# A decoder layer with product-key experts: one-hots shared out anew, search split, loads moved

## The chip, the core and the metric

The kernel runs on one core of a Trainium2 chip. The metric is the device time of one launch in microseconds (us); lower is better. Before the change it is 3035.75 us (median of 3 runs, 3030.55 to 3037.25).

## The reference

One decoder layer over 1024 tokens of width 1024. Two head groups (multi-scale retention, sliding-window attention) feed an output projection and a layer norm; that part stays as it is. What matters here is the expert layer behind it:

```python
q = (xt @ w_pq).reshape(T, H, 2, PEER_HALF)               # H = 8 heads, 2 halves
s = jnp.einsum('thpd,hpkd->thpk', q, sub_keys)            # 128 keys a half
s1, i1 = lax.top_k(s[:, :, 0], K); s2, i2 = lax.top_k(s[:, :, 1], K)      # K = 16
cand = (s1[..., :, None] + s2[..., None, :]).reshape(T, H, K * K)
top_s, pos = lax.top_k(cand, K)
idx = jnp.take_along_axis(cand_idx, pos, axis=-1)         # i1 * 128 + i2: one of 16384 experts
g = jax.nn.softmax(top_s, axis=-1)
a = gelu(einsum('cd,ced->ce', x, u_tab[idx])) * g         # 128 experts for each token
y = einsum('ce,ced->cd', a, v_tab[idx])
h = layer_norm(ALPHA * h + y, ln2_w, ln2_b)
```

## The kernel before, in words

Five stages follow each other, each with one instruction stream per engine and a meeting of all engines at its end: `project`, `attend`, `score` (product-key scores), `experts_in` (stage four, L1033) and `experts_out` (stage five, L1414). The order of the work is written out by hand; semaphores join the engines, and every engine and queue runs in order.

Instead of gathering 128 rows of u and v for every token, the kernel computes z = u h for all 16384 experts, densely, for five of the eight token blocks (blocks 3 to 7; `ZT` = 640 columns), and a dense gate matrix for six blocks (`GATE_BLOCKS`). The three other blocks get their z by gathered rows of u: GpSimd issues an indirect DMA for each slot, VectorE forms the dot product of the row with h (`dot`, L1360). Two of these blocks gather rows of v in stage five too.

Stage four has eight turns (`for s in range(TB)`) of 32 slots. A slot is half a u tile of 128 experts: TensorE runs 24 matmuls over 384 columns (first half) or 256 columns (second half) of `z_half` (L1178 to 1180). For each tile ScalarE rounds u (`split_u`, L857), GpSimd subtracts (L861), ScalarE copies both halves of z out of PSUM (L1249) and issues the store (L1252). Over that three jobs are spread:

- turns 0 to 5: the search of one token block a turn on VectorE, in pieces (`top_piece`): `side` twice and `pairs` for each head (top 16 of 128, then of 80 sums), `decode` and `names` for two heads. `names` compares (L818), multiplies by the index tables (L822, two instructions of 512 columns) and reduces (L824). `pairs` begins with four small additions (L788). The last heads of blocks 0 and 1 are searched ahead of turn 0.
- all turns: the dots, `PER_TURN` of them in each turn. `gather` runs four slots ahead of `dot` in a ring of six.
- turns 2 to 7: the gate matrix of one block a turn, 32 steps of four tokens in the slots after the first. In a step VectorE makes two one-hots by comparing an iota in PSUM with the expert's two names (`make_hot`, L1348, 1024 columns), ScalarE scales one of them by the gate (`scale_hot`, L1220, four instructions of 128 columns), TensorE multiplies them (L1188) and ScalarE copies the product out (`take_gates`, L1231), storing it every eight steps (L1236). The names and gates of a block come transposed through PSUM in a turn's slot 0 (L1203) and are copied out by VectorE in slot 1 (L1387).

In slot k ScalarE runs, in this order: the split (even slots), the copy of z, the store (odd slots), `scale_hot` of the slot's step, `take_gates` of the step of slot k - 1. TensorE multiplies a step's one-hots behind the half tile of the next slot.

Stage five has 32 rounds. A round takes four rows of z and of v: ScalarE applies Gelu, rounds a and v (L1598, L1603), VectorE multiplies by the gates and forms the low parts (L1707, L1711, L1733), TensorE adds 144 matmuls into y (L1568 to 1570). GpSimd gathers 320 rows (L1638) for VectorE (`add_row`, `dot_row`) in a ring of four. Its first gather waits for the z and gates of round 1 (`pool.wait_ge(z_here[1], 32)`). SP loads v rows 2 and 3, then z and gates of round 1, then h for the cycled blocks, h for the gathered blocks, and v of round 1.

Of the kernel before, what the change touches and what calls it, by code (L numbers as in the profile page):

```python
# [1 line left out]

# [93 lines left out]

def project(nc, d, room):
# [7 lines left out]
    with ExitStack() as ctx:  # L105
        sb, bank, sem = memory(nc, ctx)
        x_raw = room.x_raw
        x_hi = sb("x_hi", [P, KT, T], F32R)
        x_lo = sb("x_lo", [P, KT, T], F32R)
        w_raw = sb("w_raw", [P, KT, 512])  # L110
        w_hi = sb("w_hi", [P, 2, KT, 512], F32R)
        w_lo = sb("w_lo", [P, 2, KT, 512], F32R)
        rope = sb("rope", [P, TB, 2, RD // 2])
        rope64 = sb("rope64", [P, TB, 2, SD // 2])
        t_cos = sb("t_cos", [P, 512])
        t_sin = sb("t_sin", [P, 512])
        res = sb("res", [P, OUT, 512])
# [164 lines left out]
class Ahead:  # L282
# [3 lines left out]
    def __init__(self, nc, ctx):  # L286
        sb, _, sem = memory(nc, ctx)
        self.room = sb("room", [P, 2 * GROUP * T + 2 * D])
        self.taken = 0
# [25 lines left out]
        self.v_here = [sem(f"v_here{e}") for e in range(2)]  # L315
        self.gelu_in, self.prod_in = sem("gelu_in"), sem("prod_in")

    def carve(self, *shape):

        n = int(np.prod(shape))  # L320
        piece = self.room[:, self.taken:self.taken + n]
        self.taken += n
        names = "abc"[:len(shape)]
        return piece.rearrange(f"p ({' '.join(names)}) -> p {' '.join(names)}", **dict(zip(names, shape)))


def attend(nc, d, hT_hi, hT_lo, room, spent):


    with ExitStack() as ctx:  # L330
# [3 lines left out]
        decayT, xi = sb("decayT", [P, RH, P]), sb("xi", [P, RH, P])  # L334
        zeta = sb("zeta", [P, RH])
        masks = sb("masks", [P, 2, 2 * P])
        gn_w, sinks = sb("gn_w", [P, RW]), sb("sinks", [P, QH])
        ln_w, ln_b = sb("ln_w", [P, D]), sb("ln_b", [P, D])
# [5 lines left out]
        rqT, rqxT, rkT = sb("rqT", [P, RH, P]), sb("rqxT", [P, RH, P]), sb("rkT", [P, RH, P])  # L344
        sqT = sb("sqT", [P, QH // 2, P])
        skT = sb("skT", [P, 2, P])
        v_prev = room.carve(SKV)
        kz = sb("kz", [P, RH, P])
        retT = sb("retT", [P, RH, P])
        state = sb("state", [P, RH, P])  # L350
# [394 lines left out]
class TopK:  # L745
# [67 lines left out]
    def names(self, link, b, two):  # L813
# [3 lines left out]
        hs = slice(2 * two, 2 * two + 2)  # L817
        link(nc.vector.tensor_tensor(self.pick[:], bc(self.ab[:].rearrange("p a h k -> p a (h k)"), 3, TOPK),  # L818
                                     bc(bc(self.places[:], 1, 2 * TOPK), 1, 2), ALU.is_equal))
        for a in range(2):  # L820
            pick = self.pick[:, a].rearrange("p (h k) c -> p h k c", k=TOPK)
            last = nc.vector.tensor_tensor(pick, pick, bc(self.top_i[:, b % 2, a, hs], 2, TOPK), ALU.mult)  # L822
# [1049 lines left out]
```

## Time and profile before

| | us |
|---|---|
| median of 3 runs | 3035.75 |
| profiled execution | 3034.71 |
| its span, first to last instruction | 3032.9 |
| TensorE busy | 2833.3 (93%) |
| VectorE busy | 2353.9 (78%) |
| ScalarE busy | 1172.3 (39%) |
| GpSimd busy | 1160.3 (38%) |
| mean DMA rate | 245 GB/s |

Engines are called PE (TensorE), PEld (its weight loads), DVE (VectorE), ACT (ScalarE), POOL (GpSimd) and SP. A busy share is an average over stages with different limits, and issuing a DMA does not count as busy. Matmuls overlap and their ends are modelled, so a matmul's duration is longer than its distance from the next. The bracket behind a row of a timeline is the idle time before it and what ended it. Stage four runs from about 720 to 1938 us, stage five from about 1941 us to the end; turn boundaries are taken where the store of a turn's sixteenth u tile is issued.

### The profile page before, as it was taken

How to read it: one execution, taken by the hardware profiler on the slowest of the kernel's cores; microseconds unless marked ns; L12 is line 12 of the kernel's file. 1: busy time of each engine (PE TensorE's matmuls, PEld its weight loads, DVE VectorE, ACT ScalarE, POOL GpSimd, SP SyncE). 2: the span in 40 equal slices, each digit the busy share in tenths (PEclk: the TensorE clock that was granted, in tenths of full speed). 3: DMA queues.
4: the chain of work that ended last, by engine and by line, in shares of the span. 5: the costliest groups of instructions: out<-in, count | busy, mean ns of one | idle time of the engine just before them, and what ended most of it. 6: DMA issues, size and time to landing. Idle time of an engine off the chain costs nothing. (4 is left out here: it accounts for less than half of the span.)

```text
span 3032.9 us, 42916 instructions
## 1 busy us (share of the span) xinstructions
PE 2833.3 (93%) x15866; PEld 2540.8 (84%) x15866; DVE 2353.9 (78%) x4726; ACT 1172.3 (39%) x2223; POOL 1160.3 (38%) x878
## 2 busy tenths in 40 slices
PE   8997998999789999899999999879999999999998
PEld 7886886888789988888988999868888888888886
DVE  6125774567999998989898777378888888888887
ACT  3112332222122566656665768333233233333331
POOL 4113220002466544444444665233443444444441
PEclk9998999999899999999999999989999999999999
DMA  5214222223788777676777999789999999999991
GB/s 188 102 65 150 87 85 90 70 85 128 244 286 287 259 248 251 243 266 245 272 258 263 366 370 374 263 307 321 331 325 319 326 332 311 327 335 314 332 321 70
DMA packets 311484, 744.31 MB, mean 245 GB/s; under 512 B 22528, under 2 KB 136448, under 8 KB 308096
## 3 DMA queue, kind: packets, MB, share of 16 engines
q1 hardware_dynamic: 190976, 307.68, 30.8%
q0 software_dynamic: 92160, 335.59, 30.6%
q10 hardware_dynamic: 28160, 98.58, 8.1%
q8 instruction: 113, 1.85, 0.2%
q14 instruction: 75, 0.61, 0.1%
HBM read 623.26 MB, written 118.49 MB: 245 GB/s over the span
## 5 line engine op out<-in xcount | busy, mean ns | idle before, releaser
L1568 PE MATMUL y_ps<-v_hi,a_hi 128*128 128x512 f32 x1536 | 601.5, 392 | 27.5 <-DVE a_lo L1711 20.1
L1569 PE MATMUL y_ps<-v_lo,a_hi 128*128 128x512 f32 x1536 | 600.7, 391 | 0.0
L1570 PE MATMUL y_ps<-v_hi,a_lo 128*128 128x512 f32 x1536 | 600.7, 391 | 0.0
L861 POOL TENSOR_TENSOR u_lo<-u_raw,u_hi 128x1024 fp32r<-128x1024 f32 x128 | 307.8, 2404 | 618.5 <-ACT u_hi L857 618.1
L1178 PE MATMUL z_first<-hT_hi,u_hi 128*128 128x384 f32 x1024 | 360.5, 352 | 42.2 <-POOL u_lo L861 39.1
L1638 POOL DMA_INDIRECT v_rows<-in_v,room x176 | 235.8, 1340 | 343.1 <-DVE y L1694 325.2
L1568 PEld LDWEIGHTS y_ps<-v_hi,a_hi 128*128 128x128 f32 x1536 | 290.2, 189 | 89.0 <-DVE a_lo L1711 20.7
L1179 PE MATMUL z_first<-hT_lo,u_hi 128*128 128x384 f32 x1024 | 350.7, 342 | 0.0
L1180 PE MATMUL z_first<-hT_hi,u_lo 128*128 128x384 f32 x1024 | 350.0, 342 | 0.0
L1569 PEld LDWEIGHTS y_ps<-v_lo,a_hi 128*128 128x128 f32 x1536 | 290.2, 189 | 60.3
L1570 PEld LDWEIGHTS y_ps<-v_hi,a_lo 128*128 128x128 f32 x1536 | 290.0, 189 | 60.4
L1220 ACT ACTIVATE hot_g<-hot,gT 128x128 f32<-128x128 f32 x768 | 244.5, 391 | 213.4 <-DVE hot L1348 207.7
L1178 PE MATMUL z_rest<-hT_hi,u_hi 128*128 128x256 f32 x1024 | 297.1, 290 | 0.0
L1180 PE MATMUL z_rest<-hT_hi,u_lo 128*128 128x256 f32 x1024 | 289.6, 283 | 0.0
L1179 PE MATMUL z_rest<-hT_lo,u_hi 128*128 128x256 f32 x1024 | 289.6, 283 | 0.0
L1694 DVE SCALAR_TENSOR_TENSOR y<-v_rows,a_rows,y 128x1024 f32<-128x1024 f32 x176 | 225.7, 1282 | 63.2 <-DMA v_rows<-in_v,room 59.0
L1188 PE MATMUL g_ps<-hot_g,hot 128*128 128x128 f32 x1536 | 212.6, 284 | 64.2 <-ACT hot_g L1220 59.9
L1603 ACT ACTIVATE v_hi<-room 128x1024 fp32r<-128x1024 f32 x128 | 135.8, 1061 | 324.7 <-DMA room<-in_v 320.9
L1348 DVE TENSOR_TENSOR hot<-near,iT 128x1024 f32<-128x1024 f32 x192 | 233.7, 1221 | 33.9 <-PE g_ps L1188 33.5
L1188 PEld LDWEIGHTS g_ps<-hot_g,hot 128*128 128x128 f32 x1536 | 197.5, 197 | 73.3 <-ACT hot_g L1220 66.0
L1178 PEld LDWEIGHTS z_first<-hT_hi,u_hi 128*128 128x128 f32 x1024 | 200.0, 195 | 44.3 <-POOL u_lo L861 40.9
L1360 DVE CUSTOM_DVE_ANT_0 room<-room,h_ps 128x1024 f32<-128x1024 f32 x161 | 196.4, 1220 | 28.0 <-DMA room<-in_u,room 16.5
(213 smaller groups left out, 6033.0 us busy)
## 6 DMA issues: line engine op xcount, KB each, us to landing
u_raw<-in_uT SPq DMA_DIRECT2D x128, 512.0 KB, 4.5
room<-in_v SPq DMA_DIRECT2D x128, 512.0 KB, 7.1
gates<-g_sb ACTq DMA_DIRECT2D x24, 2048.0 KB, 9.8
z<-z_sb ACTq DMA_DIRECT2D x128, 320.0 KB
g_in<-gates SPq DMA_DIRECT2D x16, 1536.0 KB, 18.6
room<-gates SPq DMA_DIRECT2D x15, 1536.0 KB, 19.1
room<-z SPq DMA_DIRECT2D x16, 1280.0 KB, 7.7
z_in<-z SPq DMA_DIRECT2D x16, 1280.0 KB, 7.9
```

The costliest lines, as they stand in the source:

```text
L861: self.nc.gpsimd.tensor_tensor(self.u_lo[e][:], self.u_raw[e][:], self.u_hi[e][:].bitcast(F32), ALU.subtract).then_inc(self.u_lo_in[e], 1)
L1178: nc.tensor.matmul(o, u_hi[e][:, k], hT_hi[:, k, cols], start=(k == 0), stop=False)
L1179: nc.tensor.matmul(o, u_hi[e][:, k], hT_lo[:, k, cols], start=False, stop=False)
L1180: last = nc.tensor.matmul(o, u_lo[e][:, k], hT_hi[:, k, cols], start=False, stop=(k == KT - 1))
L1188: last = nc.tensor.matmul(g_ps[g][:, t], hot[g][:, 1, t], hot1_g[g][:, t], start=True, stop=True)
L1220: last = nc.scalar.activation(hot1_g[g][:, t], hot[g][:, 0, t], ACT.Copy, scale=gT[:, t0 + t:t0 + t + 1])
L1348: nc.vector.tensor_tensor(hot[g][:], bc(bc(iota_ps, 1, 4), 1, 2), bc(iT[:, :, t0:t0 + 4], 3, NK), ALU.is_equal).then_inc(hot_in[g], 1)
L1568: nc.tensor.matmul(o, ah, v_hi[p][:, i, c], start=(opens(r, s) and i == 0), stop=False)
L1569: nc.tensor.matmul(o, ah, v_lo[p][:, i, c], start=False, stop=False)
L1570: last = nc.tensor.matmul(o, al, v_hi[p][:, i, c], start=False, stop=(closes(r, s) and i == GROUP - 1))
L1638: nc.gpsimd.indirect_dma_start(out=rows_in[i % RING][:], out_offset=None, in_=d["u"] if table == "u" else d["v"].rearrange("a b c -> (a b) ...
L1694: nc.vector.scalar_tensor_tensor(y[:, b], rows_in[i % RING][:], a_rows[:, b, slot:slot + 1], y[:, b], ALU.mult, ALU.add).then_inc(row_used, 1)
```

## The change

- Buffers of all stages are cut out of one new tile `late`. No instruction comes or goes with that.
- One-hots: for the first five gate blocks (turns 2 to 6) VectorE makes only the second one-hot (512 columns). ScalarE makes the first one, scaled, by itself: four Abs of name minus iota, a wait for them, and four Relu of gate minus gate times that distance. VectorE copies the negated gates once a turn. The last block (`SIGNED`, turn 7) keeps the old way.
- Search: `pairs` and `names` (now `match` and `weigh`) copy one operand into PSUM and read it there; `weigh` multiplies in one instruction of 1024 columns. In `score` they stay as they were.
- The last head of block 1 is searched in slots 28 to 31 of turn 0, its gates follow in slot 0 of turn 1.
- Dots by turn, and the first slot for them, change; the first four gathers take one slot each.
- Loads: z and gates of round 1 and v rows 2 and 3 are issued at the end of stage four. Stage five's first gathers wait for none of them; v of round 1 is loaded ahead of the gathered blocks' h.

```diff
-    PER_TURN = [40, 40, 34, 34, 34, 34, 60, 44]
+    PER_TURN = [34, 40, 34, 34, 34, 34, 62, 48]
+    SIGNED = DB - 1
...
-            first, end = 6 if s == 0 else 0, 3 * SLOTS // 4 if s == TB - 1 else SLOTS
+            first, end = 8 if s == 0 else 0, 3 * SLOTS // 4 if s == TB - 1 else SLOTS
...
@@ TopK.pairs, TopK.weigh
+        if near is not None:
+            first_side = near[:, NK:NK + TOPK]
+            link(nc.vector.tensor_copy(first_side, self.top[:, 0]))
...
+            link(nc.vector.tensor_copy(top_i, self.top_i[:, b % 2, :, hs]))
+            pick = self.pick[:].rearrange("p a (h k) c -> p (a h) k c", k=TOPK)
+            link(nc.vector.tensor_tensor(pick, pick, bc(top_i.rearrange("p a h c -> p (a h) c"), 2, TOPK), ALU.mult))
...
@@ experts_in, SP: the end of the last turn
+                        sp.dma_start(ahead.g_in1[:], gates[:, :, GROUP * GT:2 * GROUP * GT]).then_inc(ahead.z1_here, 16)
+                        sp.dma_start(ahead.z_in1[:], d["z"].rearrange("n e t -> e n t")[:, GROUP:2 * GROUP]
+                                     ).then_inc(ahead.z1_here, 16)
+                        for e in range(2):
+                            sp.dma_start(ahead.late_rows[e], d["v"][2 + e]).then_inc(ahead.late_v_here[e], 16)
...
@@ experts_in, PE: gates
+                    pe.wait_ge(hot_in[g], step // 2 + 1)
                     pe.wait_ge(hot_g_in[g], step // 2 + 1)
...
@@ experts_in, ACT: scale_hot
-                    act.wait_ge(hot_in[g], step // 2 + 1)
+                    if step // SLOTS == SIGNED:
...
+                    if step % SLOTS == 0:
+                        act.wait_ge(turned, step // SLOTS + 1)
+                    wait(act, g_done[g], step // 2)
                     for t in range(4):
+                        i = t0 + t
+                        last = nc.scalar.activation(apart[g][:, t], iota[:], ACT.Abs, scale=-1.0, bias=iT[:, 0, i:i + 1])
+                    last.then_inc(own_act, 1)
+                    act.wait_ge(own_act, step + 1)
+                    for t in range(4):
+                        i = t0 + t
+                        last = nc.scalar.activation(hot1_g[g][:, t], apart[g][:, t], ACT.Relu,
+                                                    scale=minus_gT[:, i:i + 1], bias=gT[:, i:i + 1])
                     last.then_inc(hot_g_in[g], 1)
...
@@ experts_in, DVE: make_hot (not SIGNED), and slot 1 of a turn
+                        nc.vector.tensor_tensor(hot[g][:], bc(iota_ps, 1, 4), bc(iT[:, 1, t0:t0 + 4], 2, NK),
+                                                ALU.is_equal).then_inc(hot_in[g], 1)
...
+                            nc.vector.tensor_scalar(minus_gT[:], g_ps[0][:, 2], -1.0, None, ALU.mult)
...
@@ experts_out
-                load_v(0, first=2)
-                load_z(1)
                 load_h(slice(GB + 1, TB - 1), cycled_here)
+                load_v(1)
                 load_h(slice(0, GB), rows_here)
-                load_v(1)
...
-                        pool.wait_ge(z_here[1], 32)
                         for k in range(EARLY):
+                            if k == 2:
+                                pool.wait_ge(v_lo_in[0], 2)
+                                pool.wait_ge(v_lo_in[1], 2)
                             gather(k)
```

## Rows read from the trace of the kernel before

**Rows 1.** Stretches: start:end length, then PE, PEld, DVE, ACT, POOL busy; clock, DMA, GB/s.

```profile
720.50:996.00 275.50, 238.67 (x1536) 236.77 (x1536) 258.00 (x800) 62.78 (x100) 151.56 (x112) 0.93 0.79 263
996.00:1645.70 649.70, 587.57 (x4101) 580.96 (x4102) 602.18 (x1521) 393.87 (x834) 290.02 (x205) 0.96 0.72 254
1645.70:1790.30 144.60, 142.68 (x1028) 141.67 (x1028) 109.34 (x154) 100.43 (x210) 92.62 (x74) 1.00 0.96 359
1790.30:1938.40 148.10, 145.05 (x1036) 143.09 (x1035) 96.47 (x134) 100.82 (x215) 76.22 (x58) 1.00 0.89 338
1938.40:2010.00 71.60, 44.53 (x172) 35.70 (x173) 37.79 (x50) 21.41 (x31) 16.23 (x15) 0.82 0.87 313
```

**Rows 2.** Waits in turns 2 to 5: total us, times, longest.

```profile
ACT hot_g L1220 <- DVE hot L1348: 172.3, 96, 6.5
PE g_ps L1188 <- ACT hot_g L1220: 58.0, 16, 5.6
```

**Rows 3.** Groups by line, VectorE, turn 2: count, busy us, mean ns, idle before.

```profile
L1348 DVE TENSOR_TENSOR hot<-near,iT 128x1024 f32<-128x1024 f32 x32 | 39.0, 1220 | 3.6 <-PE g_ps L1188 3.5
L822 DVE TENSOR_TENSOR room<-room,top_i 128x512 f32<-128x512 f32 x8 | 9.6, 1240 | 0.1
```

**Rows 4.** Groups by line, VectorE, turn 0, the same columns.

```profile
L1360 DVE CUSTOM_DVE_ANT_0 room<-room,h_ps 128x1024 f32<-128x1024 f32 x18 | 22.0, 1221 | 1.7 <-DVE top_i L776 0.6
L788 DVE TENSOR_TENSOR room<-top 128x16 f32<-128x16 f32 (+1 forms) x40 | 9.0, 286 | 0.2
L822 DVE TENSOR_TENSOR room<-room,top_i 128x512 f32<-128x512 f32 x12 | 7.8, 689 | 0.2
```

**Rows 5.** Timeline of ScalarE within turn 2: start, us, line, operation.

```profile
1047.99 0.33 ACTq L1236 DMA_DIRECT2D gates<-g_sb  x1
1048.41 1.06 ACT L857 ACTIVATE u_hi<-u_raw 128x1024 fp32r<-128x1024 f32 x1 [0.51 <-ACT g_sb L1231]
1049.38 0.47 ACT L1249 ACTIVATE z_sb<-z_first 128x384 f32<-128x384 f32 x1
1049.79 1.28 ACT L1220 ACTIVATE hot_g<-hot,gT 128x128 f32<-128x128 f32 x4
1050.98 1.09 ACT L1231 ACTIVATE g_sb<-g_ps 128x512 f32<-128x512 f32 x1
1051.94 0.38 ACT L1249 ACTIVATE z_sb<-z_rest 128x256 f32<-128x256 f32 x1
1052.36 0.33 ACTq L1252 DMA_DIRECT2D z<-z_sb  x1
...
1054.97 1.10 ACT L1231 ACTIVATE g_sb<-g_ps 128x512 f32<-128x512 f32 x1
1055.85 1.07 ACT L857 ACTIVATE u_hi<-u_raw 128x1024 fp32r<-128x1024 f32 x1
```

**Rows 6.** One line's instructions: ns min/median/max. L829 (Exp) and L1614 (Gelu) take no pointer.

```profile
L1220 ACT ACTIVATE hot_g<-hot,gT x768: 384/388/412, 1007.1 to 1903.3; 128x128 f32<-128x128 f32 x192
L829 ACT ACTIVATE gap_e<-gap x8: 310/312/314, 730.3 to 1619.5; 128x128 f32<-128x128 f32 x8
L1614 ACT ACTIVATE a_rows<-room x1: 291/291/291, 1951.5 to 1951.5; 128x128 f32<-128x128 f32 x1
```

**Rows 7.** Timeline of TensorE within turn 6: three successive gate steps.

```profile
1702.21 1.05 PE L1188 MATMUL g_ps<-hot_g,hot 128*128 128x128 f32 x8
...
1705.98 1.05 PE L1188 MATMUL g_ps<-hot_g,hot 128*128 128x128 f32 x8
...
1711.04 1.05 PE L1188 MATMUL g_ps<-hot_g,hot 128*128 128x128 f32 x8
```

**Rows 8.** Timeline of VectorE ahead of turn 0: the four additions of one head.

```profile
724.18 0.45 DVE L788 TENSOR_TENSOR room<-top 128x32 f32<-128x32 f32 x4
```

**Rows 9.** Timelines of GpSimd and TensorE early in stage five.

```profile
1960.21 0.96 POOL L1638 DMA_INDIRECT room<-in_v,room  x1 [19.01 <-DMA g_in<-gates]
...
2008.52 0.79 PE L1568 MATMUL y_ps<-v_hi,a_hi 128*128 128x512 f32 x1 [13.96 <-DVE a_lo L1711]
```

**Rows 10.** Line L1638: time from issue to landing of a gather.

```profile
DMA to landing us min/median/max: 4.1/8.0/11.1
```

More of the change, by code:

```diff
@@ L94, in memory, with carve_late, part @@
     return sb, bank, sem
+def carve_late(room, *shapes):
+    ends = list(itertools.accumulate([int(np.prod(shape)) for shape in shapes], initial=0))
+    return [part(room.late[:, a:b], shape) for a, b, shape in zip(ends, ends[1:], shapes)]
+def part(piece, shape):
+    names = "abc"[:len(shape)]
+    return piece.rearrange(f"p ({' '.join(names)}) -> p {' '.join(names)}", **dict(zip(names, shape)))
 def project(nc, d, room):
@@ L1187, in gates @@
                     for t in range(4):
-                        last = nc.tensor.matmul(g_ps[g][:, t], hot[g][:, 1, t], hot1_g[g][:, t], start=True, stop=True)
+                        last = nc.tensor.matmul(g_ps[g][:, t], hot[g][:, t], hot1_g[g][:, t], start=True, stop=True)
                     last.then_inc(g_done[g], 1)
@@ L1300, in _ @@
                             pool.wait_ge(ahead.s_stored, 16 * PH)
-                            for i in range(EARLY):
-                                gather(i)
+                        if s == 0 and 4 <= k < 4 + EARLY:
+                            gather(k - 4)
                         for i in own_rows(s, k):
@@ L1335, in top_piece @@
                         else:
-                            tk.pairs(link, b, h)
+                            tk.pairs(link, b, h, near)
                             if h == PH - 1:
@@ L1433, in experts_out @@
         y = sb("y", [P, TB, D])
-        rows_in = ahead.rows + [sb(f"v_rows{i}", [P, D]) for i in range(RING - len(ahead.rows))]
+        rows_in = ahead.rows + [sb("v_rows", [P, D])] + ahead.late_rows
         a_rows = sb("a_rows", [P, GB, PH * TOPK])
@@ L1439, in experts_out @@
         y_ps = [bank(f"y_ps{n}") for n in range(8)]
-        z_here = [sem(f"z_here{p}") for p in range(2)]
+        z_here = [sem("z0_here"), ahead.z1_here]
         v_here = ahead.v_here
@@ L1484, in closes, with raw @@
             return r == NG - 1 or (s not in HELD and run(r, s) < LAST * (r + 1))
+        def raw(r, i):
+            return ahead.late_rows[i - 2] if r == 0 and i >= 2 else v_raw[i % 2]
         def made(r):
@@ L1529, in load_z, with load_v @@
                         z_here[p], 16)
-                def load_v(r, first=0):
-                    for i in range(first, GROUP):
-                        wait(sp, v_lo_in[i % 2], 2 * r + i // 2)
+                def load_v(r):
+                    for i in range(GROUP):
+                        wait(sp, v_lo_in[i % 2], 1 if r == 1 and i < 2 else 2 * r + i // 2)
                         sp.dma_start(v_raw[i % 2][:], d["v"][GROUP * r + i]).then_inc(v_here[i % 2], 16)
```

150 lines of the change are left out of this document (90 added, 60 removed).

## The prediction

> **What bounds the kernel now.** I read the busy shares by stretch first, then the waits, the groups by line, and the timelines at the places that these named. The change touches stage four and the opening of stage five; the allocation into one tile issues nothing, so stages one to three cost what they cost. In turns 0 and 1 VectorE is busy 258.0 of 275.5 us, and in turns 2 to 5 602.2 of 649.7 us, 162.4 us a turn; TensorE has idle time beside it [rows 1]. Turn 6 has no search: there VectorE is busy 109.3 of 144.6 us, while TensorE is busy 142.7 us at full clock [rows 1]. So 144.6 us is what a turn with a gate block takes when TensorE sets it, and turns 2 to 5 lose 17.8 us each to VectorE. The waits say how: ScalarE waits 172 us for VectorE's one-hots, and TensorE 58 us for the scaled ones [rows 2]. ScalarE itself has room, 98.5 us busy a turn [rows 1]. The change takes from VectorE and gives to ScalarE, so the question is whether ScalarE still has room when it is done.
>
> **VectorE in turns 2 to 6.** A turn has 32 steps; a one-hot instruction falls from 1024 columns, 1.22 us [rows 3], to 512, for which the uncontended product shows 0.69 us [rows 4]: 32 x 0.53 = 17.0 us less. The four pairs of products, eight at 1.24 us [rows 3] (0.69 in turn 0 [rows 4], so they lose time to something else in these turns), become four of 1024 columns at 1.22 plus a small copy, say 0.2: 3.9 us less. Turns 2 to 5 then hold 150.5 - 20.9 = 129.6 us of work, and with the 11.9 us that VectorE idles in such a turn now, 142 us. That is under TensorE's 144.6 us: VectorE stops being the bound.
>
> **ScalarE in turns 2 to 6.** What a tile (two slots, two steps) takes when ScalarE waits for nobody is read start to start [rows 5]: split 0.97, copy 0.41, one-hots 1.19, gates out 0.96, copy 0.42, store 0.42 (as from the gates store to the next split), and for the second step 1.19 and 0.88, with a quarter of a gates store 0.10. Sum 6.54 us; 16 tiles make 104.6 us, room beside 144.6.
>
> A new step: four Abs with one pointer operand, as the four Copy today, 1.28 us to their end [rows 5]; then a wait for their results, for which the nearest row is the 0.04 us from the end of a copy (1051.94 + 0.38) to the store that waits for it [rows 5]; then four Relu with two pointers, scale and bias. One pointer costs 388 - 312 to 388 - 291 = 76 to 97 ns against the same width without [rows 6], about 87. No row shows two. If the second is paid like the first, Relus follow each other at 0.30 + 0.087 = 0.385 us, four take 1.54; if it is free, 1.19. I take 1.54, the nearest row being the price of the first pointer. A step is then 2.86 us instead of 1.19, 1.67 more, and a turn 104.6 + 32 x 1.67 = 158.0 us.
>
> To this comes a gap at each turn's start, since the names of the next block come only after the last product. From the end of the last scaled one-hot TensorE still has a gate block, a wide half, transposes, and a narrow half. Gate block and narrow half are 3.77 us, gate block and wide half 5.06 [rows 7]; with 0.5 for transposes, and 0.8 for ScalarE's copy and store, less the second gate block's 1.05, 9.1 us, against 5.7 us of work that ScalarE has in the meantime (three gates out, two stores and three copies, one split, from the same rows 5). The gap is 3.4 us. With the Exp of 0.31 [rows 6] a turn takes **161.7 us**. ScalarE becomes the bound.
>
> Turns 2 to 5: 4 x 161.7 = 646.8 against 649.7 [rows 1], **-2.9 us**. The seventeen microseconds that VectorE gives up are spent on ScalarE. Turn 6, which VectorE did not hold, goes from 144.6 to 161.7, **+17.1 us**. The doubled wait on TensorE's gate products costs nothing, since VectorE's half is ready first; behind Abs and Relu on ScalarE stand the gates out and the next split, and GpSimd waits for the split, but ScalarE's own sum already counts that.
>
> The Trainium skill, page "ScalarE: Activation LUTs", section "What ACT_TABLE_LOAD costs", says that each such pointer operand adds about 93 ns and that neighbours overlap by about 93 ns. The traces show that for the first pointer only. By it an estimate for the Relus is 1.55 us and the end 3037 us; the case of a free second pointer (below) would be out.
>
> **Turns 0 and 1.** VectorE sets them and does not wait, so only its work counts, not its place: searching block 1's last head later is worth nothing by itself. Six dots fewer at 1.22 [rows 4]: -7.3. The forty additions of turn 0 take 9.0 us [rows 4]; undisturbed a group of four takes 0.45 [rows 8], ten groups 4.5, plus ten copies of 16 columns at some 0.2 (between 0.11, a quarter of that group, and the 0.29 mean of the additions): -2.5. The products: six of 1.22 and a copy against 7.8 us [rows 4], +0.7, and +0.2 in turn 1. Sum **-8.9 us**, between -4 (the copies twice as dear and more, and the dots' gathers starting later) and -14 (part of the 37 us that TensorE idles there [rows 1] goes too). GpSimd's first gathers, one a slot, no longer hold up its u tiles.
>
> **Turn 7.** It keeps the old one-hots and gets four more dots. VectorE has room (96.5 of 148.1 us), the DMAs less: 0.89 busy at 338 GB/s [rows 1]. Four rows are 2.1 MB, 6.2 us at that rate; hidden, 0. I take **+3 us**. Two more in turn 6 find room in the longer turn. The loads added at its end (1.3 + 1.5 + 1.0 MB, four instructions on SP) stand behind the last gates load, when no gather runs any more; SP has nothing else queued. If that cover is gone, 3.8 MB at 338 GB/s are 11 us.
>
> **The opening of stage five.** Until 2010 us TensorE is busy 44.5 of 71.6 us [rows 1]. The first gather waited 19.0 us for round 1's loads and started at 1960.2; the last long wait of TensorE, for round 1's low parts, ends at 2008.5 [rows 9]. VectorE stands between them: ten gathered rows in round 1, each landing 8.0 us after its issue [rows 10] in a ring of four. With the gathers freed at once and round 1's z and v early, VectorE begins that round sooner, but is stopped by the gathered blocks' h, which SP now loads behind v of round 1, whose last row waits for VectorE. Bounds: 0 (h eats it all) and -19 (the gathers' whole head start); half way, a landing of 8 us, is **-8 us**. Behind it TensorE sets the stage as before.
>
> **Sum.** -8.9 - 2.9 + 17.1 + 3 - 8 = +0.3 us on the profiled execution's 3034.71 (span 3032.9 and 1.8 around it): 3035.0. The median of the runs lies 1.0 above that execution; I say **3035**. A difference of 0.2%, 6 us, is what a measurement of this kernel can tell from none.
>
> **The rivals.**
> - *The second pointer is free.* Step 2.51, +1.32; a turn 104.6 + 42.2 + 3.7 = 150.5, say 151 with VectorE and TensorE close behind: turns 2 to 5 -45.7, turn 6 +6.4, the rest -13.9, together -53: **2982**. For it: only that no row shows two. Chance 0.16.
> - *Slower: the wait between Abs and Relu is dear.* ScalarE must let its last Abs land before the first Relu, 160 times. My 0.04 us is from a store behind a copy, not from an arithmetic instruction behind its own kind. At 0.20 it adds 160 x 0.16 = 26: **3061**. It decides from 0.08 us on. Against it: the four Copy of today follow each other without any such gap [rows 5], but none of them reads the one before. Chance 0.13.
> - *The loads' order bites*: h holds VectorE, nothing won in stage five, turn 7 pays 6: **3046**. Chance 0.05.
> - *More is won beside the one-hots*: -14 and -19 in place of -8.9 and -8: **3019**. Chance 0.08.
>
> My own case has 0.58, within 15 us of 3035: 0.19 of it faster by over 0.2%, 0.22 within, 0.17 slower. Faster 0.19 + 0.16 + 0.08 = 0.43, same 0.22, slower 0.17 + 0.13 + 0.05 = 0.35. The range 2985 to 3061 leaves out the lower part of the first rival, the upper part of the second, and some 0.03 more.
>
> **What would show it.** Right: ScalarE busy over 0.9 in turns 2 to 6, all five near 162 us, turn 6 longer than before; TensorE waiting for the scaled one-hots in small pieces; VectorE under 135 us in turns 2 to 5. Four Relus at 1.6 us or 1.28 settle the pointer; from the last Abs to the first Relu, the wait. Wrong: turn 6 still near 145 us, or turns 2 to 5 near 150.

## The result, and the profile after

The changed kernel takes **3040.09 us**, median of 20 runs (3036.5 to 3041.49), against 3032.86 of the kernel before on the same chip (20 runs): ratio 1.0021, interval 1.0014 to 1.0028. It is slower by 7 us, little, but clear of noise. 3035 and "no change" were forecast; the time lies in the range that was given. A slower kernel had a chance of 0.35 there.

The first view of the changed kernel is the busy time by stretch: start:end length, then PE, PEld, DVE, ACT, POOL busy, granted clock, DMA share, GB/s. A turn ends with its last z store, as in [rows 1]; the stretches are turns 0 and 1, turns 2 to 5, turn 6, turn 7, and the opening of stage five.

```profile
719.10:981.70 262.60, 237.29 (x1536) 235.09 (x1536) 245.02 (x805) 62.78 (x100) 145.35 (x106) 0.95 0.79 264
981.70:1634.95 653.25, 591.99 (x4101) 579.43 (x4101) 524.27 (x1562) 587.28 (x1346) 292.67 (x205) 0.98 0.72 252
1634.95:1801.10 166.15, 151.26 (x1028) 148.19 (x1028) 95.93 (x159) 149.00 (x338) 96.79 (x78) 0.96 0.89 326
1801.10:1953.90 152.80, 147.06 (x1035) 144.81 (x1035) 98.86 (x136) 100.94 (x215) 78.14 (x60) 0.99 0.96 360
1953.90:2020.00 66.10, 45.37 (x179) 36.52 (x180) 39.24 (x51) 21.10 (x32) 19.33 (x16) 0.85 0.79 284
```

Read it beside [rows 1]. In turns 2 to 5 VectorE falls from 602.2 to 524.3 us busy and ScalarE rises from 393.9 to 587.3: the load has changed engines, and the time has not fallen. Turn 6 goes from 144.6 to 166.2. By terms, on the two profiled executions (spans 3032.9 and 3039.3, 6.4 apart; the terms come from boundaries rounded to 0.1):

| | forecast | measured |
|---|---|---|
| turns 0 and 1 (first to last z store 266.0 to 253.1, and the stage starts 1.4 earlier) | -8.9 | -14.3 |
| turns 2 to 5 (649.7 to 653.3) | -2.9 | +3.6 |
| turn 6 (144.6 to 166.2) | +17.1 | +21.6 |
| turn 7 (148.1 to 152.8) | +3 | +4.7 |
| stage five (1094.5 to 1085.4) | -8 | -9.1 |
| sum | +0.3 | +6.5 |

Of the first term, 1.4 is no gain that can be told from scatter: the first z store lies anywhere between 726.1 and 730.5 us in the profiled executions of this document. From the first to the last z store of the two turns it is -12.9.

Next, ScalarE's timeline within turn 4 (start, us, line, operation, and in brackets the idle time before and what ended it), which answers to [rows 5], and the two new lines' durations, ns min/median/max, which answer to [rows 6].

```profile
1331.34 1.08 ACT L1280 ACTIVATE late<-g_ps 128x512 f32<-128x512 f32 x1
1332.22 1.05 ACT L880 ACTIVATE u_hi<-u_raw 128x1024 fp32r<-128x1024 f32 x1
1333.18 0.47 ACT L1298 ACTIVATE z_sb<-z_first 128x384 f32<-128x384 f32 x1
1333.54 1.27 ACT L1264 ACTIVATE late<-room,late 128x128 f32<-128x128 f32 x4
1334.85 1.65 ACT L1269 ACTIVATE late<-late,minus_gT 128x128 f32<-128x128 f32 x4
1336.40 1.05 ACT L1280 ACTIVATE late<-g_ps 128x512 f32<-128x512 f32 x1
1337.26 0.41 ACT L1298 ACTIVATE z_sb<-z_rest 128x256 f32<-128x256 f32 x1
1337.70 0.33 ACTq L1301 DMA_DIRECT2D z<-z_sb  x1
1338.07 1.28 ACT L1264 ACTIVATE late<-room,late 128x128 f32<-128x128 f32 x4 [0.40 <-ACT z_sb L1298]
1339.39 1.65 ACT L1269 ACTIVATE late<-late,minus_gT 128x128 f32<-128x128 f32 x4
1340.94 1.10 ACT L1280 ACTIVATE late<-g_ps 128x512 f32<-128x512 f32 x1
```

```profile
L1264 ACT ACTIVATE late<-room,late x640: 383/389/409, 994.8 to 1797.9; 128x128 f32<-128x128 f32 x160
L1269 ACT ACTIVATE late<-late,minus_gT x640: 477/481/498, 996.2 to 1799.5; 128x128 f32<-128x128 f32 x160
```

In this stretch ScalarE has no idle time but the 0.40 behind a store. A step, from the first Abs to the next gates out, is 1338.07 to 1340.94, 2.87 us (2.86 forecast). A Relu takes 481 ns against an Abs's 389: the second pointer costs 92 ns, like the first. The Trainium skill's rule on pointer operands (page "ScalarE: Activation LUTs", section "What ACT_TABLE_LOAD costs"), about 93 ns for each, is borne out for the second. A whole tile, two steps, is 1331.34 to 1340.94, 9.60 us.

Now the start of turn 4 on ScalarE and on TensorE, and the same place by stretch. The one-hots of turn 3's last step end at 1307.71; the first Abs of turn 4 starts at 1319.76.

```profile
1306.06 1.65 ACT L1269 ACTIVATE late<-late,minus_gT 128x128 f32<-128x128 f32 x4
1307.61 1.04 ACT L1280 ACTIVATE g_sb<-g_ps 128x512 f32<-128x512 f32 x1
...
1315.71 0.49 ACT L1298 ACTIVATE z_sb<-z_first 128x384 f32<-128x384 f32 x1 [2.91 <-PE z_first L1213]
1318.91 0.38 ACT L1298 ACTIVATE z_sb<-z_rest 128x256 f32<-128x256 f32 x1 [2.71 <-PE z_rest L1213]
1319.33 0.33 ACTq L1301 DMA_DIRECT2D z<-z_sb  x1
1319.76 1.28 ACT L1264 ACTIVATE late<-room,late 128x128 f32<-128x128 f32 x4 [0.46 <-ACT z_sb L1298]
```

```profile
1304.95 1.13 PE L1222 MATMUL g_ps<-late 128*128 128x128 f32 x8 [0.55 <-issue]
1308.79 1.25 PE L1222 MATMUL g_ps<-late 128*128 128x128 f32 x8 [2.71 <-ACT g_sb L1280]
1309.70 0.67 PE L1211 MATMUL z_first<-hT_hi,u_hi 128*128 128x384 f32 x1
1310.16 0.52 PE L1212 MATMUL z_first<-hT_lo,u_hi 128*128 128x384 f32 x1
1310.48 0.52 PE L1213 MATMUL z_first<-hT_hi,u_lo 128*128 128x384 f32 x1
...
1314.12 0.33 PE L1212 MATMUL z_first<-hT_lo,u_hi 128*128 128x384 f32 x1
1314.29 0.33 PE L1213 MATMUL z_first<-hT_hi,u_lo 128*128 128x384 f32 x1
...
1315.51 0.49 PE L1237 MATMUL g_ps<-ident,found 128*128 128x128 f32 x3
```

```profile
1304.10:1308.80 4.70, 1.44 (x12) 1.11 (x10) 4.42 (x13) 4.67 (x12) 2.85 (x4) 1.00 0.75 258
1309.70:1312.70 3.00, 3.00 (x11) 3.00 (x11) 0.00 (x0) 2.49 (x3) 0.00 (x0) 0.50 0.98 388
```

This gap at the start of turn 4 is 12.05 us where the prediction had 9.1. TensorE's last gate block starts 1.08 after the last one-hot, behind the gates out of an earlier step (2.71 us of wait). TensorE was busy 1.44 of the 4.7 us before; then its granted clock is 0.50, the lower of its two levels (1.2 of 2.4 GHz), matmuls follow each other at 0.32 instead of 0.17 us, and the wide half takes 5.81 us (1309.70 to 1315.51). ScalarE waits 2.91 us for it and 2.71 us for the narrow half, 5.6 us. A turn is then 16 x 9.60 + 4 gates stores of 0.65 + Exp with its idle 0.6 + 5.6 = 162.4 us, the measured length of turn 4.

The other turn starts look alike, and some are worse. The gaps ahead of turns 3, 4, 5 and 6 are 11.85, 12.05, 13.14 and 13.53 us. In turns 3, 5 and 6 the gate block, too, runs at half clock, 1.70 us to the wide half instead of 0.91. In the kernel before, the clock is 1.00 and the wide half takes 4.25 to 4.28 us at each of these places; here it takes 4.83, 5.81, 6.12 and 6.19. By these durations the half clock costs 1.4, 1.5, 2.6 and 2.7 us, 8 us in four turns, about as much as the whole kernel is slower. The rows are gate block and wide half of turn 4 before, and of turn 6 after:

```profile
1320.00:1327.20 7.20, 7.20 (x51) 7.08 (x51) 5.87 (x16) 5.22 (x9) 1.92 (x2) 1.00 0.99 359
1634.85:1642.74 7.89, 7.89 (x32) 7.86 (x33) 0.00 (x0) 3.23 (x4) 2.92 (x2) 0.63 0.94 385
```

Turn 0 on VectorE by groups (count, busy us, mean ns, idle before), which answers to [rows 4]:

```profile
L841 DVE TENSOR_TENSOR room<-room,near 128x1024 f32<-128x1024 f32 x5 | 6.1, 1220 | 0.2
L801 DVE TENSOR_TENSOR room<-near,top 128x16 f32<-128x16 f32 (+1 forms) x36 | 3.9, 172 | 0.3
L798 DVE COPY near<-top 128x16 f32<-128x16 f32 x9 | 1.6, 174 | 0.1
L839 DVE CAST near<-top_i 128x64 f32<-128x64 uint32 x5 | 1.1, 228 | 0.2
```

36 additions are 3.9 us instead of 9.0 for 40, a mean of 172 ns instead of 286; a copy to PSUM takes 0.17 or 0.23 us, about the 0.2 that was taken. Nine heads and five pairs fall into this turn now, instead of ten and six.

### The profile page after: what moved, and what is told of

It is laid out like the page before. It is cut to its first block and busy times, and to the rows that moved or that the text cites. A ratio compares the mean times of both kernels' runs of the same rounds, so it can differ in the third digit from the quotient of the medians.

```text
span 3039.3 us, 43628 instructions
## 1 busy us (share of the span) xinstructions
PE 2844.4 (94%) x15866; PEld 2543.6 (84%) x15866; DVE 2250.0 (74%) x4782; ACT 1413.6 (47%) x2863; POOL 1162.4 (38%) x878
## 5 line engine op out<-in xcount | busy, mean ns | idle before, releaser
L1222 PE MATMUL g_ps<-late 128*128 128x128 f32 x1536 | 214.7, 284 | 78.4 <-issue 48.9
L1222 PEld LDWEIGHTS g_ps<-late 128*128 128x128 f32 x1536 | 195.0, 195 | 95.8 <-issue 94.8
L1269 ACT ACTIVATE late<-late,minus_gT 128x128 f32<-128x128 f32 x640 | 264.3, 483 | 5.3
L1713 POOL DMA_INDIRECT late<-in_v,room x128 | 165.5, 1293 | 254.0 <-DVE y L1771 235.0
L1417 DVE CUSTOM_DVE_ANT_0 u_rows<-u_rows,h_ps 128x1024 f32<-128x1024 f32 x159 | 194.0, 1220 | 40.0 <-DMA u_rows<-in_u,room 25.7
L1264 ACT ACTIVATE late<-room,late 128x128 f32<-128x128 f32 x640 | 204.2, 392 | 28.9 <-ACT z_sb L1298 25.6
```

The lines of the kernel that those rows point to most:

```text
L1222: last = nc.tensor.matmul(g_ps[g][:, t], hot[g][:, t], hot1_g[g][:, t], start=True, stop=True)
L1264: last = nc.scalar.activation(apart[g][:, t], iota[:], ACT.Abs, scale=-1.0, bias=iT[:, 0, i:i + 1])
L1269: last = nc.scalar.activation(hot1_g[g][:, t], apart[g][:, t], ACT.Relu, scale=minus_gT[:, i:i + 1], bias=gT[:, i:i + 1])
L1417: nc.vector.tensor_tensor_reduce(rows_in[r][:], rows_in[r][:], h_ps[:], 1.0, 0.0, ALU.mult, ALU.add, ahead.z_rows[:, b, slot:slot + 1]).th ...
L1713: nc.gpsimd.indirect_dma_start(out=rows_in[i % RING][:], out_offset=None, in_=d["u"] if table == "u" else d["v"].rearrange("a b c -> (a b) ...
```

## Experiments

Each ratio is to the kernel before, on the same chip, with its 95% interval. Lengths of turns come from one profiled execution of each kernel; the wide half at the start of turn 3, for one, takes 4.83 us in the changed kernel and 5.98 and 6.06 in e6 and e15, whose ScalarE and TensorE run the same instructions there, so single turns differ by a us or two without a cause in the edit.

| run | us | ratio, interval | turns 0+1 | turns 2 to 5 | turn 6 | turn 7 | stage five |
|---|---|---|---|---|---|---|---|
| before | 3032.9 | 1 | 266.0 | 649.7 | 144.6 | 148.0 | 1094.5 |
| the change | 3040.1 | 1.0021 [1.0014, 1.0028] | 253.1 | 653.3 | 166.2 | 152.8 | 1085.4 |
| e1 | 2991.5 | 0.9858 [0.984, 0.9877] | 253.1 | 619.3 | 150.5 | 153.5 | 1085.7 |
| e2 | 2978.6 | 0.9816 [0.9798, 0.9834] | 253.1 | 604.8 | 154.1 | 151.8 | 1085.4 |
| e3 | 3016.4 | 0.9945 [0.9927, 0.9963] | 253.1 | 635.8 | 159.5 | 151.4 | 1084.5 |
| e8 | 3056.8 | 1.0067 [1.0046, 1.0088] | 265.5 | 655.4 | 166.0 | 149.6 | 1092.8 |
| e13 | 3037.9 | 1.0017 [1.0008, 1.0025] | 253.1 | 653.1 | 163.6 | 151.7 | 1085.8 |
| e7 | 3026.7 | 0.9984 [0.9975, 0.9992] | 253.1 | 645.3 | 163.8 | 148.6 | 1085.3 |
| e17 | 3024.0 | 0.9967 [0.9955, 0.9979] | 253.1 | 636.8 | 160.0 | 158.1 | 1085.9 |
| e5 | 2976.4 | 0.9806 [0.9791, 0.9821] | 253.0 | 604.3 | 147.2 | 157.6 | 1084.1 |
| e15 | 3044.9 | 1.0036 [1.0024, 1.0049] | 257.7 | 655.3 | 165.9 | 151.7 | 1084.0 |
| e14 | 3043.5 | 1.0037 [1.0023, 1.005] | 262.1 | 654.5 | 165.7 | 148.7 | 1085.3 |
| e6 | 3036.5 | 1.0012 [1.0003, 1.0021] | 250.1 | 656.1 | 165.8 | 151.1 | 1084.6 |
| e11 | 3045.6 | 1.0049 [1.0035, 1.0063] | 253.0 | 653.4 | 165.7 | 150.9 | 1091.6 |
| e12 | 2978.2 | 0.9827 [0.9814, 0.9841] | 253.0 | 614.7 | 147.5 | 151.5 | 1081.4 |
| e16 | 2972.3 | 0.9798 [0.9784, 0.9811] | 253.1 | 605.8 | 149.6 | 153.8 | 1079.0 |

**e1, the old one-hots in all turns.**

```diff
-    SIGNED = DB - 1
+    SIGNED = 0
...
-                    if step // SLOTS == SIGNED:
+                    if step // SLOTS >= SIGNED:
...
```


> The changed kernel with the one-hots of all six gate blocks made by VectorE and scaled by ScalarE, as before; everything else of the change stays. Theory (ScalarE's own length sets turns 2 to 6 of the changed kernel): turn 6 falls from 166 us back to about 145, turns 2 to 5 fall from 163.3 to about 157, where VectorE (129 us busy now, 17 more for the wide one-hots, some 12 idle) sets them; in all about 3040 - 21 - 25 = 2994 us. Rival (turn 6 is long because of its two more dots and the DMAs, and turns 2 to 5 because of what happens at a turn's start): turn 6 stays above 158 us and the kernel above 3020.

2991.5: the rest of the change is worth 41 us when left alone, the one-hots cost 49 on top of it. 30 of the 41 are in turns 2 to 5, 154.8 us each: VectorE, still their bound, is 27.8 us less busy there. This part of the gain is what ScalarE's bound hides in the changed kernel. Turn 6 comes back to 150.5 us, not to the 145 expected; VectorE waits 28.5 us for gathered rows there, 25.6 before, and the rest was not tried. The row of turns 2 to 5:

```profile
982.10:1601.40 619.30, 584.66 (x4101) 578.70 (x4102) 574.39 (x1558) 393.69 (x834) 288.98 (x204) 0.98 0.73 265
```

**e8, the one-hots alone, in the kernel before.** The diff is the change's own for the scaled one-hots and the halved VectorE ones; all else is as before.

> The kernel before with only the one-hots of turns 2 to 6 made anew (four Abs, a wait, four Relu on ScalarE, half the one-hot on VectorE), nothing else of the change. Theory: turns 2 to 5 about as before, 162 to 164 us, now set by ScalarE; turn 6 from 145 to 163 or more: about 3033 + 4 + 19 = 3056 us. Rival (VectorE's relief is worth its 17 us in turns 2 to 5 and ScalarE only fills gaps): 3033 - 60 + 5 = 2978 us.

3056.8, 25 us slower: turn 6 +21.4, turns 2 to 5 +5.7. The two halves of the change do not add (-41 and +25 would be -16, not +7): with ScalarE as the bound, all that relieves VectorE in turns 2 to 5 is worth next to nothing (655.4 us without it, 653.3 with it).

**e2, one pointer in Relu.** The gates lie between 0 and 1, so Relu(g - d) is the scaled one-hot as well, and nothing of the computation is left out (the expectation below says otherwise, wrongly).

```diff
-                                                    scale=minus_gT[:, i:i + 1], bias=gT[:, i:i + 1])
+                                                    scale=-1.0, bias=gT[:, i:i + 1])
```


> The changed kernel with an immediate scale of -1 in the four Relus in place of the pointer to the negated gates; left out is the scaling of the first one-hot by the gate. Theory: each Relu loses one pointer, 0.09 to 0.1 us, 0.39 us a step; a tile on ScalarE falls from 9.60 to about 8.8 us, TensorE's own 8.83 us is reached, turns 2 to 5 come down from 163.3 to about 151 and turn 6 from 166 to 153: about 3040 - 60 = 2980 us. Rival (the second pointer is not what makes the step long, or ScalarE is not the bound): less than 15 us off, above 3025.

2978.6, a complete kernel that beats both the changed one and the one before. Its Relu, and its turns 2 to 5:

```profile
L1269 ACT ACTIVATE late<-late x640: 384/387/405, 994.6 to 1737.5; 128x128 f32<-128x128 f32 x160
```

```profile
980.10:1584.90 604.80, 576.84 (x4101) 571.64 (x4101) 518.52 (x1562) 541.67 (x1346) 290.21 (x205) 0.99 0.77 272
```

94 ns less for each of 640 Relus are 60 us; 61.5 came off. In turns 2 to 5 it is 48.1 for 512 Relus, and 48.5 came off. TensorE is now busy 576.8 of 604.8 us there, but ScalarE still waits for nobody inside its tiles, which take 8.90 us: the two engines are nearly level, and which of them is the bound is not shown.

**e3, Relu without the wait for Abs.** It reads the row of numbers instead of Abs's result, so the comparison with the index is left out.

```diff
-                    last.then_inc(own_act, 1)
-                    act.wait_ge(own_act, step + 1)
...
-                        last = nc.scalar.activation(hot1_g[g][:, t], apart[g][:, t], ACT.Relu,
+                        last = nc.scalar.activation(hot1_g[g][:, t], iota[:], ACT.Relu,
```


> The changed kernel with Relus that read the iota in place of the distance, so that they need not wait for the Abs; left out is the comparison in the first one-hot. Theory: the wait costs what the trace shows between the start of the last Abs and the first Relu, 0.42 us, less the 0.30 at which such instructions follow each other: 0.12 to 0.13 us a step, 160 steps, about 20 us: 3020 us. Rival (the wait costs only the 0.04 us of my sum, the rest is hidden): 6 us, 3034.

3016.4 (four runs, 3012.2 to 3019.6). 23.7 us over 160 steps are 0.15 a step; the changed kernel's timeline has 0.12 (from the start of the last Abs to that of the first Relu 0.42 us, between two Abs 0.30).

**e13, the gates out moved ahead of the last one-hot.** This tests the first explanation of the long gap.

```diff
+                        done = list(steps_at(s, k - 1))
                         for step in steps_at(s, k):
                             scale_hot(step)
-                        for step in steps_at(s, k - 1):
+                            if done:
+                                take_gates(done.pop(0))
+                        for step in done:
                             take_gates(step)
```


> The changed kernel with one move on ScalarE: in a gate slot that holds two steps (the middle one and the last one of a turn) the gates of the step before are taken out between the two one-hots, not behind both. Same work. Theory (what went wrong in the forecast is the start of a turn, not the steps: the last gate block of TensorE stands 2.7 us waiting for gates out that are queued behind the last one-hot, so ScalarE's own gap there is about 6.4 us and not 3.4): the 2.7 us go, less the 1.0 us of gates out that no longer fills ScalarE's gap, five turns: 1.5 to 2.5 us a turn, 3030 to 3033 us, ratio to before 0.999 to 1.000. Rival (the gap has nothing to do with that order; steps and contention alone make the turn 1.6 us longer than forecast): stays within 3 us of 3040, ratio 1.002.

3037.9: turns 2 to 5 stay what they were (-0.2 together), and the explanation falls. Turn 6 alone is 2.6 shorter; 1.4 of that is a half clock that lasts less long there (a wide half of 4.79 us, not 6.19), the rest is not resolved. TensorE's last gate block now waits for the one-hot itself, which the gates out have pushed back by what they took:

```profile
1307.96 1.65 ACT L1269 ACTIVATE late<-late,minus_gT 128x128 f32<-128x128 f32 x4
```

```profile
1309.71 1.13 PE L1222 MATMUL g_ps<-late 128*128 128x128 f32 x8 [2.55 <-ACT late L1269]
```

**e17, the old one-hots in the last two steps of turns 2 to 6.** The second explanation: TensorE idles behind two one-hots that ScalarE makes in a row, and pays with its clock.

```diff
+        def by_act(step):
+            return step // SLOTS < DB - 1 and step % SLOTS < SLOTS - 2
...
-                    if step // SLOTS == SIGNED:
+                    if not by_act(step):
...
```


> The changed kernel with the old one-hots in the last two steps of turns 2 to 6 alone (VectorE makes both, ScalarE only scales them), the other thirty by Abs and Relu. Theory (the start of a turn is too long because TensorE idles ahead of its last gate block, behind ScalarE's last one-hots, and then computes the next wide half partly at half clock: 1.5 us of the 12.1 us gap): ScalarE saves 2 x 1.54 = 3.1 us of steps a turn, the half clock's 1.5 us go too, five turns of 4.6 us: 3015 to 3019 us, ratio 0.994 to 0.9955. Rival (the gap keeps its length, only the two steps are saved): 3.1 us a turn, 3023 to 3027 us, ratio 0.997 to 0.998.

The time, 3024.0, is the rival's; the trace says why. Turns 3 to 6 fall by 4.3, 3.9, 5.5 and 6.2 us: the 3.1 us of the two steps, and 1.2, 0.8, 2.4 and 3.1 more, against the 1.4, 1.5, 2.6 and 2.7 that the half clock cost there. That is the theory's mechanism, but turn 2 falls by 2.8 only and turn 7 gives 5.3 back. The same place in this kernel, and TensorE ahead of it and in the wide half:

```profile
1298.19 2.44 ACT L1259 ACTIVATE late<-late 128x128 f32<-128x128 f32 x8
1307.08 0.49 ACT L1301 ACTIVATE z_sb<-z_first 128x384 f32<-128x384 f32 x1 [1.23 <-PE z_first L1217]
...
1311.12 1.28 ACT L1267 ACTIVATE late<-room,late 128x128 f32<-128x128 f32 x4 [0.46 <-ACT z_sb L1301]
```

```profile
1295.90:1300.60 4.70, 4.70 (x40) 4.70 (x39) 2.64 (x4) 4.70 (x13) 2.44 (x2) 1.00 0.42 166
1302.60:1306.80 4.20, 4.20 (x27) 4.20 (x26) 3.03 (x12) 2.74 (x3) 1.98 (x3) 1.00 0.98 330
```

TensorE is busy all of the 4.7 us ahead, the clock is 1.00 all through the wide half, here and at the other four turn starts, and the gap is 1300.63 to 1311.12, 10.5 us, 1.6 shorter. From the last one-hot to the wide half it is 2.0 us in both kernels, so the 1.6 are the clock's. In turn 7 ScalarE waits for VectorE's one-hots 25.7 us, against 17.8 in the changed kernel, and VectorE for gathered rows 14.5 against 11.5; e5 shows a long turn 7 as well. So the one-hots come late behind the dots there; why more than before was not tried.

**e7, gates out between Abs and Relu.**

```diff
...
                         for step in steps_at(s, k):
-                            scale_hot(step)
+                            scale_hot(step, 0)
                         for step in steps_at(s, k - 1):
                             take_gates(step)
+                        for step in steps_at(s, k):
+                            scale_hot(step, 1)
```


> The changed kernel with ScalarE's order within a step turned to Abs, gates out of the step before, Relu, so that the wait between Abs and Relu lies beside other work. Nothing is left out. Theory (the wait costs 0.13 us of 160 steps, as the kernel without it showed, and the last gate block's wait for gates out goes with it): 21 us for the wait, some 5 to 10 for the start of a turn: 3010 to 3020 us, ratio 0.992 to 0.996. Rival (ScalarE then waits for TensorE's products before the Relus instead, a new wait in the old one's place): 3030 us or more, ratio 0.999 or more.

3026.7, between the two. The wait between Abs and Relu is hidden, but a tile is 9.51 instead of 9.60 us, not 9.34: in each tile ScalarE now waits for TensorE's wide half, which starts later behind the later Relus.

```profile
1332.42 0.49 ACT L1303 ACTIVATE z_sb<-z_first 128x384 f32<-128x384 f32 x1 [0.16 <-PE z_first L1213]
```

**e5, ScalarE makes two steps of three.**

```diff
+        def by_act(step):
+            return step // SLOTS < DB - 2 and step % 3 != 1
...
-                    if step // SLOTS == SIGNED:
+                    if not by_act(step):
...
```


> The changed kernel with the gate work shared out: in turns 2 to 5 ScalarE makes the scaled one-hots of two steps of three by Abs and Relu, VectorE makes both one-hots of the third as before; turn 6 has the old one-hots throughout, as turn 7. Theory (ScalarE's sum alone sets turns 2 to 6; with a third of it gone VectorE and TensorE are just under 150 us, as in the kernel with one pointer): turns 2 to 5 at 149 to 153 us instead of 163, turn 6 at 150 as with old one-hots throughout: 3040 - 48 - 16 = 2976 us, between 2968 and 2988, ratio 0.979 to 0.985. Rival (each change between the two ways costs a hand-over between VectorE and ScalarE): turns of 158 and more, 3005 us or more, ratio 0.991 or more.

2976.4, the theory's time: turns 2 to 5 at 151.1 us on average and turn 6 at 147.2, with TensorE busy 0.96 and 0.97 of them, more than any other engine; turn 7 is longer.

**e15, the names in SBUF again.** The argument `near` is left out of the calls.

```diff
-                            tk.pairs(link, b, h, near)
+                            tk.pairs(link, b, h)
...
-                        tk.weigh(link, b, q, near)
+                        tk.weigh(link, b, q)
```


> The changed kernel with the sums and products of the search reading the names in SBUF again, without the copies to PSUM (the first part of the change undone alone). Theory (that part is what made the first two turns 4 to 5 us shorter than the forecast's terms say, and in turns 2 to 6, which ScalarE sets, it is worth nothing): 3.4 us of additions come back in each of turns 0 and 1, the products cost what they did: 4 to 9 us slower than the changed kernel, 3044 to 3049 us, ratio 1.0035 to 1.005. Rival (the copies eat what the additions win; the first turns owe their time to the fewer dots and to TensorE's smaller idle time): within 3 us of 3040, ratio 1.002.

3044.9: turns 0 and 1 get 4.6 longer. VectorE's groups in turn 0 of this kernel say by what:

```profile
L845 DVE TENSOR_TENSOR room<-room,top_i 128x512 f32<-128x512 f32 x10 | 8.6, 896 | 0.2
L801 DVE TENSOR_TENSOR room<-top 128x16 f32<-128x16 f32 (+1 forms) x36 | 6.2, 235 | 0.1
```

The additions cost 2.3 us more than in the changed kernel, the products 2.5 (896 ns each, not the 689 of [rows 4]), the copies' 1.6 and 1.1 are saved: 2.1 us, and about as much in turn 1 (2.2 us longer). The names through PSUM are worth 4.6 us in these turns, not the 1.6 of the forecast.

**e14, the dots shared out as before.**

```diff
-    PER_TURN = [34, 40, 34, 34, 34, 34, 62, 48]
+    PER_TURN = [40, 40, 34, 34, 34, 34, 60, 44]
```


> The changed kernel with the dots shared among the turns as before (40, 40, 34, 34, 34, 34, 60, 44 instead of 34, 40, 34, 34, 34, 34, 62, 48), the rest of the change kept. Theory (VectorE sets turn 0, six dots at 1.22 us are all of 7.3 us there; turn 7 with four rows fewer gives 2 to 4 us back): turn 0 at 123 us instead of 115.6, turn 7 at 149 to 151 instead of 152.8: 3042 to 3046 us, ratio 1.003 to 1.0045. Rival (turn 0 is short because TensorE stands less, not because of the dots): turn 0 within 3 us, the whole not above 3040, ratio 1.002 or less.

3043.5. Turn 0 is 7.4 longer, as six dots at 1.22 us say, turn 1 is 1.6 longer, turn 7 is 4.1 shorter. The profiled execution is the longest of the five (3048.3 us), so the 9.0 of turns 0 and 1 may be a little high.

**e6, the search in one part, ahead of turn 0.**

```diff
...
+                for b in range(2):
+                    for n in range(3):
+                        last_head(b, n)
+                    last_head(b, 3)
...
-                            if s == 0 and k >= TOPK_SLOTS:
-                                last_head(1, k - TOPK_SLOTS)
```


> The changed kernel with the search of block 1's last heads back ahead of turn 0, so in one part as before; the rest of the change kept. Theory (VectorE sets turns 0 and 1 and what stands ahead of them, so only how much it does counts, not where): the first z store comes later by what turn 0 is shorter, 3037 to 3043 us, ratio 1.001 to 1.003. Rival (searching later lets TensorE and GpSimd start sooner and is worth some microseconds by itself): 3045 us or more, ratio 1.004 or more.

3036.5, 3.6 us below the changed kernel, a little outside what the theory allowed; the intervals overlap. In the profiled execution turns 0 and 1 are 250.1 us instead of 253.1, turn 1 alone 122.7 instead of 137.5, but turns 2 to 5, where the half clock lasts longer this time, are 2.8 longer. Searching in two parts wins nothing; it costs 3 us in turns 0 and 1 of this execution, and whether it costs the whole kernel anything is not shown.

**e11, the four loads back in stage five.**

```diff
+                for e in range(2):
+                    sp.dma_start(ahead.late_rows[e], d["v"][2 + e]).then_inc(ahead.late_v_here[e], 16)
+                load_z(1)
                 load_h(slice(GB + 1, TB - 1), cycled_here)
```


> The changed kernel with the four loads (gates, z and two parts of v of round 1) back at the opening of stage five, the rest of the change kept. Theory (the 9.1 us that stage five is shorter come from these loads being early; in turn 7 they cost at most 2 us): stage five 7 to 10 us longer, 3045 to 3050 us, ratio 1.004 to 1.006. Rival (stage five is shorter for the room that the change gives, gathered rows freed at once, and not for the loads): within 3 us of 3040, ratio 1.001 to 1.003.

3045.6: stage five is 6.2 us longer, turn 7 1.9 shorter. The loads make two thirds of stage five's gain.

**e12 and e16, what the runs point to, put together.** Both have e2's Relu, the old one-hots in turn 6, and h of the gathered blocks ahead of v of round 1; e12 has e7's order too.

```diff
...
-    SIGNED = DB - 1
+    SIGNED = DB - 2
...
-                load_v(1)
                 load_h(slice(0, GB), rows_here)
+                load_v(1)
```


> The changed kernel put together from what the other runs point to: Relu with one pointer (scale -1, bias the gate), the gates of the step before taken out between Abs and Relu, turn 6 with the old one-hots as turn 7, and h of the gathered blocks loaded ahead of v of round 1 at the opening of stage five. Nothing is left out. Theory (with one pointer TensorE sets turns 2 to 5 at about 150 us, turn 6 goes from 154 to 150, stage five gains 0 to 5 us): 2966 to 2975 us, ratio 0.978 to 0.981, the fastest of all. Rival (TensorE's bound leaves nothing for the other edits): the 2978 us of the kernel with one pointer alone, ratio 0.9816.

> As the last kernel put together, but with ScalarE's order as the change has it (Abs, Relu, gates of the step before): Relu with one pointer, turn 6 with the old one-hots, h of the gathered blocks ahead of v of round 1. Nothing is left out. Theory (the turned order makes TensorE wait for the scaled one-hots where TensorE is the bound, 153.7 us a turn against 151.2 with one pointer alone; the other two edits are worth 6.6 and 4 us): 2965 to 2971 us, ratio 0.977 to 0.980. Rival (the order has nothing to do with it, turn 6 and stage five give nothing back): 2976 to 2980 us, ratio 0.981 or more.

2978.2 and **2972.3**. The turned order costs 8.9 us in turns 2 to 5, where TensorE and ScalarE are nearly level: in most tiles ScalarE waits for the wide half again (0.28 at the place shown below), and a tile is 9.11 us, 8.90 in e2. e16 is the fastest median, 2.0% below the kernel before; its interval overlaps e5's. In it stage five is 6.4 us shorter than in the changed kernel. The first wait below is e12's, the second the changed kernel's in stage five, for h; in e16 VectorE no longer waits there.

```profile
1206.00 0.49 ACT L1303 ACTIVATE z_sb<-z_first 128x384 f32<-128x384 f32 x1 [0.28 <-PE z_first L1213]
```

```profile
1987.91 0.29 DVE L1762 TENSOR_TENSOR a_rows<-a_rows,room 128x128 f32<-128x128 f32 x1 [5.99 <-DMA y<-h]
```

## Why the prediction was wrong

**The mechanism was right.** ScalarE is the bound of turns 2 to 6. What e2 takes from its Relus in turns 2 to 5, 48.1 us, comes off as 48.5; with a third of the steps back on VectorE (e5) these turns fall to 151 us; and the one-hots alone make turn 6 long (e8). VectorE's busy time, 131 us a turn, was forecast at 129.6; the step at 2.86 and measured at 2.87, its second pointer and its wait included. The first rival (a free pointer) is out by the Relu's 481 ns, the second (a dear wait) by the 0.12 to 0.15 us of e3, which are inside the step as it was priced. Of the signs, the longer turn 6 and four Relus at 1.65 us came as named; ScalarE is busy 0.90, not over it, and TensorE waits in long pieces, 2.7 us, at the turn starts.

**The step that failed is the gap at a turn's start**, put at 9.1 us with 3.4 of them idle. In turn 4 it is 12.05, with 5.6 idle. The prediction took the gate block to start when the one-hots end, and all of TensorE's work at full clock, from turn 6 of the kernel before, where TensorE hardly stood and its clock was 1.00 [rows 1, rows 7]. Once ScalarE is the bound, TensorE stands ahead of that gate block: 1.1 us are the gates out in front of it, 1.5 us the half clock behind it (5.81 against 4.28 us for the wide half in e2, where the clock stays at 1.00 at this place), and some 0.4 are not resolved. In turns 5 and 6 the half clock is 2.6 and 2.7 us. It is shown by e17, whose turns get back about what it cost; that TensorE's idle time brings it on rests on the rows ahead of it, 1.4 of 4.7 us busy here and 4.7 of 4.7 in e17. The 1.1 us can't be had by reordering (e13).

In turns 2 to 5 an error the other way hides most of this: in turn 4 the idle time is 2.2 us more than forecast, gates stores 1.0 and Exp 0.3, but sixteen tiles of 9.60 us instead of 9.78 take 2.9 back, and the turn is only 0.7 longer than 161.7. Turn 3 is 0.8 longer. Turn 5 is 2.0 longer, by its longer gap, and turn 2 is 3.0 longer; it has no such gap, but TensorE waits 3.6 us for a low part of u at its start. Together 6.5 us of the error.

**Turn 6** has the same gap, longer (waits of 3.36 + 3.05 us), and the Gelu with its table load, 1.28 + 0.21 us, which stood beside idle time before and is now on the bound's path: +21.6 instead of +17.1. The prediction left the Gelu out of the sum.

**Turn 7** was forecast at +3, measured +4.7. e14 and e11 undo its two parts: four more dots 4.1, the loads 1.9, together more than the whole.

**Turns 0 and 1**: -14.3 instead of -8.9, or -12.9 without the earlier start, which is scatter. The dots are worth up to 9.0 instead of 7.3, the names 4.6 instead of 1.6; the search in two parts, forecast at nothing, took some 3 back. That makes 10.6; some 2 us have no owner. The forecast priced the additions in turn 0 alone and the old products at their undisturbed 0.69 us; in the new order these would have cost 0.9 in both turns (e15).

**Stage five**: -9.1 against -8. Both halves of the reasoning are seen: the loads (e11), and the stop for h behind v of round 1, 5.99 us. But half way between 0 and -19 was a choice, and that it came so close is luck.

So two terms erred by about 11 us up (turns 2 to 6), one by 5 down. That the total missed by 6 us only is luck, too. The forecast of no change stood on a sum of terms of both signs, three of them larger than the 6 us that a measurement tells from none; it could not be that sharp.

## What to carry to other kernels

Before moving work to an engine with idle time, add up that engine's own turn, and then the round trip with the engine that it feeds at the places where both stop; the idle time that this makes on TensorE can be paid twice, in the wait and in the clock after it (1.1 and 1.5 us in turn 4). On ScalarE a second per-partition pointer can cost more than moving the work brings (here 61 us, where the move without it brings 13, e1 to e2): look for an immediate in its place. When several parts of a change relieve engines in the same turns, only the part that relieves the bound counts: -41 and +25 made +7 here.

## What the runs showed of the hardware

- A second pointer operand costs an ACTIVATE of 128 columns 92 ns (389 with one, 481 with two); with an immediate in its place it takes 387 again (e2).
- An ACTIVATE that waits for the one before it on the same engine started 0.42 us after that one's start, against 0.30 without the wait.
- After a stretch with TensorE busy 1.44 of 4.7 us the granted clock was 0.50 for about 3 us (turn 4 of the changed kernel); in the same place of e17, with TensorE busy 4.7 of 4.7 us, it stayed at 1.00. In e2, busy 2.4 of 4.7 us, it stayed at 1.00 at the starts of turns 4 and 5 and fell at those of turns 3 and 6.
- VectorE's additions of 16 and 32 columns took a mean of 172 ns with one operand in PSUM and 235 with both in SBUF, in the same place (e15); a product of 1024 columns with one operand in PSUM kept 1.22 us, two of 512 with both in SBUF took 0.69 to 0.94 each.
